# One level of seven-product multiplication in the MLP of a hybrid decoder step, in two token groups

## The reference

```python
x = x + gt1 * rmsnorm(y, lw['n1_post'])
h = rmsnorm(x, lw['n2_pre']) * (1.0 + sc2) + sh2
u = jnp.square(jax.nn.relu(h @ lw['w_up'])) @ lw['w_down']
x = x + gt2 * rmsnorm(u, lw['n2_post'])
```

## Time and profile before

| | value |
|---|---|
| median of two runs | 2032.28 us |
| span of the profiled execution | 2028.2 us |
| PE busy | 1907.2 us, 94% |
| PE weight loads busy | 1614.4 us, 80% |
| DVE busy | 697.8 us, 34% |
| ACT busy | 599.7 us, 30% |
| POOL busy | 387.4 us, 19% |
| PE's share of the chain that ended last | 82% |
| mean granted clock of PE | 0.985 |

### The profile page before, as it was taken

How to read it: one execution, slowest core, us unless ns; L and a number is a source line. 1 busy time by engine, 2 the same in 40 slices (tenths; PEclk the granted TensorE clock), 3 DMA queues, 4 the chain that set the end, 5 groups by cost and what they waited for, 6 DMA issues and landing times.

```text
span 2028.2 us, 32352 instructions
## 1 busy us (share of the span) xinstructions
PE 1907.2 (94%) x12832; PEld 1614.4 (80%) x12832; DVE 697.8 (34%) x907; ACT 599.7 (30%) x869; POOL 387.4 (19%) x427
## 2 busy tenths in 40 slices
PE   4988989789999999999999999999999999999987
PEld 2777867566898887777777778989899999999977
DVE  3634243444543552111113454222323132222235
ACT  5545444332332432011012232223222222222211
POOL 2222021232110112100000142303040303131202
PEclk9999999899999999999999999999999999999999
DMA  8111012287122023333231531211111111111132
GB/s 287 32 34 43 22 43 70 96 291 258 53 54 54 22 63 98 100 96 93 74 92 55 155 120 54 67 42 42 41 43 51 41 41 41 42 51 41 42 120 89
DMA packets 137685, 159.95 MB, mean 79 GB/s; under 512 B 10697, under 2 KB 111354, under 8 KB 136442
## 3 DMA queue, kind: packets, MB, share of 16 engines
q1 hardware_dynamic: 119568, 104.94, 16.8%
q0 software_dynamic: 15776, 46.68, 7.6%
q10 hardware_dynamic: 2250, 7.04, 1.0%
HBM read 142.72 MB, written 15.91 MB: 78 GB/s over the span
## 4 chain that ended last, share of the span: by engine, by line
PE 82%; DVE 4%; issue 3%; DMA 3%; ACT 3%; SPq 2%; POOL 1%; POOLq 1%; PEld 1%; ACTq 0%; DVEq 0%; PEldq 0%
PE psum L272 42%; PE psum L2238 17%; PE psum L2085 6%; PE psum L2132 4%; PE psum L1822 2%; PE psum L1835 1%; DMA work<-in_cache_k 1%; DVE nmax L1317 1%; ACT work L968 1%; PE psum L2187 1%; DMA work<-in_ada_w 1%; PE psum L1903 1%; SPq L452 1%; PE psum L2059 1%; PE psum L1897 1%
## 5 line engine op out<-in xcount | busy, mean ns | idle before, releaser
L272 PE MATMUL psum<-h_hi,w_hi 128*128 128x288 f32 (+1 forms) x1776 | 400.4, 334 | 3.9 <-DVE w_lo L260 2.9
L272 PE MATMUL psum<-h_hi,w_lo 128*128 128x288 f32 (+1 forms) x1776 | 394.0, 330 | 0.0
L272 PE MATMUL psum<-h_lo,w_hi 128*128 128x288 f32 (+1 forms) x1776 | 393.9, 330 | 0.0
L272 PEld LDWEIGHTS psum<-h_hi,w_hi 128*128 128x128 f32 x1776 | 269.3, 189 | 41.0 <-issue 10.1
L260 DVE TENSOR_TENSOR w_lo<-w_raw,w_hi 128x1024 fp32r<-128x1024 f32 x108 | 165.6, 1533 | 380.6 <-ACT w_hi L254 373.4
L272 PEld LDWEIGHTS psum<-h_lo,w_hi 128*128 128x128 f32 x1776 | 269.9, 188 | 28.4
L272 PEld LDWEIGHTS psum<-h_hi,w_lo 128*128 128x128 f32 x1776 | 269.8, 188 | 28.5
L835 POOL TENSOR_TENSOR work<-work 128x1088 f32<-128x1088 f32 x56 | 142.6, 2546 | 514.4 <-ACTq L1157 514.4
L2238 PE MATMUL psum<-u_hi,w_lo 128*128 128x288 f32 (+1 forms) x672 | 148.4, 328 | 0.0
L2238 PE MATMUL psum<-u_lo,w_hi 128*128 128x288 f32 (+1 forms) x672 | 148.4, 328 | 0.0
L2238 PE MATMUL psum<-u_hi,w_hi 128*128 128x288 f32 (+1 forms) x672 | 148.4, 328 | 0.0
(11 more groups left out here) (367 smaller groups left out, 2338.4 us busy)
## 6 DMA issues: line engine op xcount, KB each, us to landing
w_raw<-in_w_in SPq DMA_DIRECT2D x44, 512.0 KB, 3.9
work<-in_cache_k SPq DMA_DIRECT2D x64, 256.0 KB, 5.9
work<-in_cache_v POOLq DMA_DIRECT2D x64, 256.0 KB, 4.9
work<-in_ada_w POOLq DMA_DIRECT2D x32, 512.0 KB, 4.1
w_raw<-in_w_mlp_up SPq DMA_DIRECT2D x32, 512.0 KB, 4.0
w_raw<-in_w_mlp_down SPq DMA_DIRECT2D x32, 512.0 KB, 3.4
work<-in_ada_w SPq DMA_DIRECT2D x8, 1024.0 KB, 16.0
out<-work POOLq DMA_DIRECT2D x12, 512.0 KB, 4.2
```

What stands on the lines that cost most here:

```text
L272: last = nc.tensor.matmul(out[:, a:b], w, m[:, k, a:b], start=(k == 0 and w is wh and m is h_hi), stop=(k == KD - 1 and w is wl))
```

## The change

The MLP's two matrix products become one level of a Strassen scheme (seven products for a 2 x 2 block product instead of eight, in the form with intermediate sums). The 1088 tokens are cut into two groups of 544. A group is worked completely, up and down, before the next, so all MLP weights are loaded twice. In a group the tokens are two halves of H = 272 columns, and the outputs and the contraction are in two halves as well.

The work is a list of 64 jobs, 32 up ("U") and 32 down ("D"), each of seven products. A product is 4 row tiles x 3 splits = 12 matmuls of 272 columns. For each job:

- SP loads 2 x 512 KB of weights into one of two slots of `mw_raw`, when DVE has finished all low parts of the job that used the slot.
- POOL makes four sums of 512 columns of weights (`sum_upper`), two sums of 272 columns of product results (`u2_and_p5`, `u3_and_p5`), and either four sums of 272 columns of the new hidden values (`combine`, after a U job) or one of 1088 columns into `yT` (`add_output`, after a D job; in the first block of a group it is a copy).
- ACT converts seven weight tiles of 512 columns, copies products 0 and 1 out of PSUM, and after a U job converts the hidden values (816 and 1088 columns).
- DVE makes seven low parts of 512 columns (`weight_low`), adds products 2 to 6 from PSUM to SBUF (`output`, 272 columns each), and for a U job does the squared Relu of 1088 columns in one instruction and the low parts of the hidden values (`up_low`, 816 and 1088 columns).

Weight parts go round a ring of five, and PE's outputs round six banks. The pieces of `h` are made for the first group between the norm's steps of phase 6 (POOL sums four of 1088 columns and makes two low parts) and for the second group in jobs 29 to 31 (DVE sums four and makes seven low parts). The second group's part of `h` is parked in DRAM. The residual is stored straight into the output, and the MLP's result is added to it by DMAs from POOL's queue that accumulate. The merged tiles are converted in two pieces each instead of one, and the order of the token tiles in phase 6 puts the samples before tile 4. Several semaphores are merged, with no effect on order.

Core of the diff (loops and helpers that hold only addresses are left out):

```diff
@@ order of jobs
+        def job_list():
+            for g in range(2):
+                yield "U", g, 0, 0
+                for b in range(NHB):
+                    for p in range(1, 4):
+                        yield "U", g, b, p
+                    if b < NHB - 1:
+                        yield "U", g, b + 1, 0
+                    for p in range(4):
+                        yield "D", g, b, p
@@ block.sync
+            def load_weights(q):
+                kind, g, b, p = JOBS[q]
+                if q >= 2:
+                    sp.wait_ge(mw_lo, 7 * (q - 1))
+                for half in (1, 0):
...
+                    sp.dma_start(mw_raw[q % 2][:, half, :, :], src).then_inc(mw_landed[q % 2], 16)
@@ block.gpsimd
-            def add_down(it, j):
-                pool.wait_ge(down_copied, KD * it + j + 1)
-                nc.gpsimd.tensor_add(yT[:, j, :], yT[:, j, :], down[j % 2]).then_inc(down_free, 1)
+            def sum_upper(q, j):
+                done = 7 * (q - 1) + (2, 3, 5, 6)[j]
+                raw = mw_raw[q % 2]
+                pool.wait_ge(mw_landed[q % 2], 32 * (q // 2 + 1))
+                if q:
+                    pool.wait_ge(mw_lo, done)
...
+                nc.gpsimd.tensor_tensor(w_sum[j], a, b, op).then_inc(mw_summed, 1)
+            def combine(q):
+                _, g, b, p = JOBS[q]
+                pool.wait_ge(u_squared, up_count(g, b, p) + 1)
+                for dst, a, b in ((4, 0, 1), (5, 2, 0), (6, 2, 4), (7, 3, 6)):
+                    nc.gpsimd.tensor_sub(u_new[:, dst, :], u_new[:, a, :], u_new[:, b, :])
+                    if dst != 4:
+                        pool.drain()
+                pool.sem_inc(u_combined, 1)
+            def u2_and_p5(q):
+                pool.wait_ge(dve_read, 6 * q + 1)
+                pool.wait_ge(act_cp, 2 * q + 2)
+                cells = job_copy[q % 2]
+                nc.gpsimd.tensor_add(cells[:, C12, :], job_u2[q % 2], cells[:, C22, :])
+                pool.drain().then_inc(pool_cp, 1)
...
+            for q in range(NQ):
...
+                if q + 1 < NQ:
+                    sum_upper(q + 1, 2)
...
+                if q and JOBS[q - 1][0] == "D":
+                    add_output(q - 1)
+                elif q and not ends_up(q - 1):
+                    combine(q - 1)
...
+                if q + 1 < NQ:
+                    sum_upper(q + 1, 3)
...
+                if q + 2 < NQ:
+                    sum_upper(q + 2, 0)
...
+                u2_and_p5(q)
+                if q + 2 < NQ:
+                    sum_upper(q + 2, 1)
...
+                u3_and_p5(q)
@@ block.vector
-                    v.tensor_mul(usq, relu[j % 2], relu[j % 2])
+            def weight_low(n):
+                dve.wait_ge(mw_hi, n + 1)
+                v.tensor_sub(ring_lo[n % RING], weight_of(n), ring_hi[n % RING].bitcast(F32)).then_inc(mw_lo, 1)
+            def output(q, i):
...
+                dve.wait_ge(prod_done, 7 * q + i + 1)
+                if i == 2:
+                    dve.wait_ge(act_cp, 2 * q + 1)
+                if i in (5, 6):
+                    dve.wait_ge(pool_cp, 2 * q + i - 4)
...
+                v.tensor_add(out, other, job_bank(7 * q + i)).then_inc(dve_read, 1)
+                if i == 6 and kind == "U":
...
+                    v.scalar_tensor_tensor(u_new[:, 0:4, :], cells, 0.0, cells, ALU.max, ALU.mult).then_inc(dve_read, 1)
+                    dve.drain().then_inc(u_squared, 1)
...
+            for q in range(NQ):
+                for i in range(7):
+                    n = 7 * q + i
...
+                    if i >= 2:
+                        output(q, i)
+                    if i in (1, 4) and finished_in(q):
+                        up_low(finished_in(q), i == 4)
...
+                    if n + RING < 7 * NQ:
+                        weight_low(n + RING)
@@ block.tensor
+                pe.wait_ge(mw_lo, n + 1)
...
+                for k in range(4):
+                    for w, low in ((ring_hi, False), (ring_hi, True), (ring_lo, False)):
+                        last = mm(out, w[n % RING][:, k, :], moving(job, i, k, low),
+                                  start=(k == 0 and w is ring_hi and not low),
+                                  stop=(k == 3 and w is ring_lo))
+                last.then_inc(prod_done, 1)
```

More of the change, by code:

```diff
@@ new lines, in build_layer, with up_count, block_end, finished_in @@
+        JOBS = list(job_list())
+        assert len(JOBS) == NQ
+        def up_count(g, b, p):
+            return 16 * g + 4 * b + p
+        def block_end(g, b):
+            return 7 * JOBS.index(("D", g, b, 3)) + 7
+        def finished_in(q):
+            for x in (q - 1, q - 5):
+                if x >= 0 and JOBS[x][0] == "U":
+                    _, g, b, p = JOBS[x]
+                    late = 5 if (p == 0 and b > 0) else 1
+                    if late == q - x and not (b == NHB - 1 and p == 3):
+                        return JOBS[x]
+            return None
@@ new lines, in first_pieces @@
+            def first_pieces(dst, a, b):
+                nc.gpsimd.tensor_sub(hp_raw[dst], a, b)
+                pool.drain().then_inc(hp_summed, 1)
+            x1_scale(3)
+            add_shift(3)
+            y_scale(5)
+            x1_scale(4)
+            add_shift(4)
+            x1_scale(5)
+            add_shift(5)
+            for j in range(4):
+                if j == 2:
+                    pool.wait_ge(y_ready, 4)
+                sum_upper(0, j)
+            y_scale(6)
+            pool.wait_ge(h_split, KD + 5)
@@ new lines, in u3_and_p5, with sample_columns @@
+            def u3_and_p5(q):
+                pool.wait_ge(dve_read, 6 * q + 3)
+                cells = job_copy[q % 2]
+                nc.gpsimd.tensor_add(cells[:, C22, :], cells[:, C22, :], cells[:, C21, :])
+                pool.drain().then_inc(pool_cp, 1)
+            def sample_columns(q):
+                for (upper, half), cell in CELL.items():
+                    pool.tensor_copy(y_samples[:, 4 * upper:4 * upper + 4, half, :], yT[:, :, cell, H - HS:H])
+                pool.drain().then_inc(fin_sample, 1)
@@ L855, in _ @@
+            add_output(NQ - 1)
+            sample_columns(NQ)
+            for f in range(NF):
+                fin_scale(1, f)
+                if f:
+                    fin_store(1, f - 1)
+            fin_store(1, NF - 1)
         @block.scalar
@@ L1710, in _ @@
+            for f in range(NF):
+                fin_tile(1, f)
         @block.tensor
@@ L2289, in _, with moving @@
[L2289 to L2291 removed]
+            up_piece = (B11, T1, T2, B21, T3, B22, T4N)
+            down_piece = ((False, 0), (True, 0), (True, 2), (False, 2), (True, 1), (False, 1), (True, 3))
+            def moving(job, i, k, low):
+                kind, g, b, p = job
+                if kind == "U":
+                    return (hp_low if low else hp_high)[up_piece[i]][:, H * k:H * k + H]
+                top, at = down_piece[i]
+                return ((ut_l if low else ut_h) if top else (ub_l if low else ub_h))[k][:, at, :]
```

859 lines of the change are left out of this document (489 added, 370 removed).

## The result

The changed kernel took 2365.52 us, median of two runs (2362.53 and 2368.50), beside 2032.28 us of the kernel before. The ratio is 1.164, with a 95% interval of 1.159 to 1.168: it is 333 us slower. Forecast were 2338 us and a range of 2170 to 2475 us. The profiled execution has a span of 2361.0 us.

A forecast was written before the change was run, and what follows sets the result against it. It took a circle of waits among DVE, SP's loads and POOL to bound the jobs at 16.6 us. 1218.8 + 15 + 1062 + 20 + 18 = 2334 us, plus 4 us to the median, gave 2338 us, range 2170 to 2475.

The forecast's parts named there:

- PE's gain: In the MLP, a 272-column matmul takes 0.1267 us and a job 10.6 us; if only PE counted, 92 us less.
- rival of 0.147 us: MLP matmuls of 272 columns take 0.147 us, so no saving though nothing else blocks: 2066 us; chance 0.03.
- exclusion: In MLP jobs, POOL sums and DVE operations with both operands in SBUF block each other but for 0.14 to 0.15 us.
- holds of 13.9 us a job: Mean time POOL and DVE hold against each other: D 12.2, U 15.6 us; 890 us over 64 jobs, a floor.
- circle: Waits from DVE's low part through SP's load and POOL's sums to DVE: D 14.9, U 18.3, mean 16.6 us.
- step from a low part to POOL's sum: In each job, SP's issue 0.24 us and landing of 2 x 512 KB 5.9 us, 6.2 us together.
- estimate of 4.4 us: Landing of a job's 1 MB of weights by the skill's page; the jobs' sum would be 96 us less.
- rival of a shorter circle: Loads land in 4.0 us, handovers hide and jobs near their 13.9 us of holds: 2166 to 2216 us; chance 0.20.
- start, middle and end: Additions outside the regular jobs: 15 us before the second product, 20 us in jobs 29 to 35, 18 us after the last product.
- sum of 2334: Whole kernel: 1218.8 + 15 + 1062 + 20 + 18 us, 306 us above the profiled execution before.
- PE's clock: Rival: a third of MLP jobs run at 1.2 GHz, 100 us more, 2438 us; chance 0.19, shared with an 8 us landing.
- PE's share: Sign in the profile after: PE's busy share in the MLP near 64%, waiting for DVE's low parts.

The follow-up runs named there:

- e2_half: Against the changed kernel, only the second of a job's two 512 KB loads is made from job 2 on, part of the computation left out: 2316.4 us.
- e1_reorder: Against the changed kernel, POOL's two weight sums that wait for a load moved behind `u2_and_p5` and `u3_and_p5`, computation complete: 2228.8 us.
- e9_no_drain: Against the changed kernel, POOL's drains in the job loop and last norms replaced by semaphores raised by the operations, order kept: 2328.1 us.
- e7_short: Against e1_reorder, POOL's weight sums and DVE's weight low parts made for only 2 of each 128 columns after the first jobs: 2017.7 us.

## Why the prediction was right, and where its terms were off

- **PE's gain** was right: 0.126 us for 272 columns against 0.1267, jobs of 10.56 against 10.6 us. The rival of 0.147 us falls. (L2532's busy time of 792.7 us over 5376 matmuls also comes to 0.147, but it counts the start-up of each lone product: 12 matmuls alone show 1.77 us, 12 within a long run 1.51.)
- **The exclusion** was right in kind and size. `weight_low` has minimum 0.676, median 0.910 and mean 1.12 us, and 693 ns at most with a PSUM operand. The holds of 13.9 us a job appeared as the measured job when the circle was opened: 14.14.
- **The circle** was right, and its sum slightly too long: D 14.5 to 14.9 us (forecast 14.9), U 17.6 (18.3), 64 x 16.21 = 1037 us where 1062 were forecast. The step from a low part to POOL's sum, 6.2 us by the forecast with a landing of 5.9, took 5.8 to 6.4 us in D jobs and 5.7 us in two U jobs (1564.47 to 1570.15, for one), so most of the 0.7 us of the U job lies there. The page's medians of 5.0 and 5.3 us (4.6 and 4.9 in this block) are for one load each, and the second of a pair is issued 0.5 us behind the first. That 5.9 fitted is in part luck: its row is the median of single loads of 256 KB out of a queue of 32 in the paged attention, where the DMA engines were busy 75 to 97%, and not of a batch of four. The estimate of 4.4 us by the Trainium skill, "DMA: Bandwidth & Descriptors", section "Anatomy of one DMA — SWDGE (gpsimd) path", which is for transfers from GpSimd's queue, is too short for this pair from SP's, which took 5.7 us or more from the issue to POOL's sum. Its sum of 96 us less overshoots for another reason too: `e2_half` shows that of a shorter landing a D job gains 1.1 us and a U job 0.2, the rest being taken by DVE's low parts and the exclusion. This the forecast, which had the landing on the path in full, did not have.
- **The rival of a shorter circle** was the right picture of what a well interleaved list gives. Its 2166 to 2216 us are just under the 2228.8 us of `e1_reorder`, as the ends were too small in both sums.
- **The steps that failed are start, middle and end**: 15, 20 and 18 us, 53 together, against 105. *Start*: the first `u2_and_p5` began at 1259.29, 3.2 us ahead of its job's end if it lies as in the last job (2324.39, the last product ending at 2327.6). That end is 1262.5 - 1218.8 - 16.2 = 27.5 us late. The first four jobs took 6 us more than four mean ones, but nearly all of that (5.5) is because they are U jobs. PE waited 10.49 us at 1254.87 for one of POOL's low parts (L980). POOL was not full ahead of it:

```profile
1245.20 1.38 POOL L907 TENSOR_SCALAR stat<-stat 128x1 f32<-128x1 f32 x1 [5.60 <-ACTq L1323]
...
1247.85 1.26 POOL L947 TENSOR_TENSOR region<-region 128x512 f32<-128x512 f32 x1
1249.26 2.04 POOL L947 TENSOR_TENSOR region<-region 128x512 f32<-128x512 f32 x1 [0.16 <-issue]
1251.27 3.45 POOL L980 TENSOR_TENSOR region_r<-region,region_r 128x1088 fp32r<-128x1088 f32 x1
```

It stood idle for 5.60 us ahead of a norm's step and then made two sums for the next job before the low part for which PE waited, so the order of its list had a part in it. I ran no version with another order there. *Middle*: 48 us instead of 20. The forecast counted busy time of DVE and POOL. It missed the stores, 17 us in all by ACT's wait for them and POOL's drains behind them, and that a last U job is followed at once by the D job that needs it. *The last jobs*: the same handover costs 7.7 us, and jobs 60 to 62 give back 14.8: some 5 because they are D jobs and so under the mean, some 10 because they have fewer sums to make. *End*: 2327.6 to 2361.0, 33.4 us instead of 18. Stores behind norms, each 4.2 us of drain, were not in it, though `e9_no_drain` shows that only 9 us of it could be saved so.
- Sum by these terms: 1218.8 + 64 x 16.21 + 27.5 + 6 + 48 + 7.7 - 14.8 + 33.4 = 2364, less 3 us by which the other regular jobs ran shorter, is the span of 2361.0. By this count the jobs came out 25 us below the forecast and the rest 52 us above it, so the sum of 2334 was missed by 27 us. About half of the error in the ends was hidden by the one in the jobs, and that is luck.
- **PE's clock** had no part in it. It was 0.93 in the eight jobs, and PE waited for others there anyway. PE's share, forecast at 64%, reads 75%, since "busy" counts the start-up of lone products; by its pace in `e7_short` it is 10.56/16.21 = 65%.

## What to carry to other kernels

Before work is moved to GpSimd, add up what its sums and VectorE's operations with two SBUF operands hold against each other: that sum, not either engine's own time, is the floor, and here it was above the whole stage before. A PSUM operand takes a VectorE operation out of that sum, even if another engine has to copy it there. In a hand-written list put what another engine waits for ahead of what waits for a load: this exchange alone was worth 137 us.

## What the hardware showed that I had not expected

- A drain on POOL behind an accumulating store that POOL issued takes 4.2 to 4.3 us instead of 0.15. A semaphore raised by the operation itself does not wait for it: in `e9_no_drain` the norms follow the stores within 0.1 us.
- A low part of 512 columns takes 0.68 us with one operand in PSUM and 0.69 with both in SBUF and POOL idle: the PSUM operand cost nothing here.
- Two mutually exclusive engines can show 92% and 89% busy in the same stretch (`e1_reorder`), because blocked time counts as busy. High shares on both are a sign of the exclusion and not of work.
